# State-space branch ahead of the attention branches, a slot table for the weights, and two modulation vectors in one tile

## The reference, cut to what matters

```python
def trunk_layer(x, mod, lp, li, ctx):
    shift1, scale1, gate1, shift2, scale2, gate2 = [mod[:, i, None, :] for i in range(6)]
    h = rmsnorm(x, lp['g_norm1']) * (1 + scale1) + shift1
    mix, new_ctx = token_mixers(h, lp, li, ctx)
    x = x + gate1 * mix
    h2 = rmsnorm(x, lp['g_norm2']) * (1 + scale2) + shift2
    x = x + gate2 * expert_choice_ffn(h2, ...)

def token_mixers(h, lp, li, ctx):
    proj = jnp.einsum('bsd,dn->bsn', h, lp['w_in'])
    # A: dense attention, B: window attention with a sink, C: state space (SSD), D: differential attention
    branches = jnp.stack([ya, yb, yc, yd], axis=2)
    up = jnp.einsum('bsnw,nwd->bsnd', branches, lp['w_br'])
    g = jax.nn.sigmoid(gate.reshape(Bz, S, N_BRANCH, D_MODEL))
    out = jnp.einsum('bsd,de->bse', jnp.sum(g * up, axis=2), lp['w_out'])
```

## Time and profile before

| what | us |
|---|---|
| median of three runs | 2039.87 (2039.13 to 2042.09) |
| the profiled execution, its own time | 2045.24 |
| its span | 2043.5 |
| PE busy | 1894.9 (93% of the span) |
| DVE, ACT busy | 482.6, 351.9 |
| mean granted TensorE clock | 0.97 |

### The profile page before, as it was taken

One profiled execution on the slowest core, in us unless ns is written; L12 is line 12 of the kernel. 1 busy time (PEld: TensorE's weight loads), 2 busy tenths in 40 slices (PEclk: granted clock), 3 DMA queues, 4 the chain that ended last, 5 costly groups with the idle time before them and its releaser, 6 DMA issues.

```text
span 2043.5 us, 19689 instructions
## 1 busy us (share of the span) xinstructions
PE 1894.9 (93%) x7750; PEld 866.6 (42%) x7750; DVE 482.6 (24%) x1249; ACT 351.9 (17%) x916; POOL 50.1 (2%) x91
## 2 busy tenths in 40 slices
PE   6999999999799999898879999999897999999988
PEld 2464444455333433333345644444554334334322
DVE  1033224453411111101020522243524001111101
ACT  2123222421210100100021232223213001001000
POOL 2100000000300000000000000000000000000000
PEclk8999999988899999999989999999888999999999
DMA  9142113245589999999951411133436899999997
GB/s 379 62 158 79 49 55 124 73 179 204 224 339 418 420 428 429 428 428 428 423 231 62 175 62 62 42 124 135 178 143 247 346 426 424 428 428 428 427 429 308
DMA packets 65476, 532.98 MB, mean 261 GB/s; under 512 B 6688, under 2 KB 6816, under 8 KB 41344
## 3 DMA queue, kind: packets, MB, share of 16 engines
q1 hardware_dynamic: 62256, 527.59, 63.1%
q0 software_dynamic: 3152, 4.47, 0.7%
HBM read 529.16 MB, written 2.88 MB: 260 GB/s over the span
## 4 chain that ended last, share of the span: by engine, by line
PE 77%; DMA 15%; DVE 4%; ACT 2%; issue 1%; SPq 0%; ACTq 0%; DVEq 0%
PE bank L588 73%; DMA ring<-in_w_e 14%; PE bank L597 4%; DMA ring<-in_w_ada 1%; ACT scr L1413 1%; DVE x L1919 0%; DVE scr L1624 0%; DVE hT L1487 0%; DVE scr L1856 0%; DVE scr L1853 0%; DVE hT L1485 0%; DVE scr L1794 0%; ACT scr L1400 0%; ACT scr L1402 0%; DVE scr L1788 0%
## 5 line engine op out<-in xcount | busy, mean ns | idle before, releaser
L588 PE MATMUL bank<-ring,hT 128*128 128x512 f32 (+2 forms) x1440 | 597.2, 568 | 2.6 <-DVE hT L1487 2.6
L588 PE MATMUL bank<-ring,scr 128*64 128x512 f32 (+1 forms) x2176 | 529.2, 598 | 44.6 <-DMA ring<-in_w_e 26.3
L588 PE MATMUL bank<-scr 128*64 128x512 f32 (+6 forms) x2048 | 437.2, 520 | 8.1 <-DVE dsm L1763 4.7
L588 PEld LDWEIGHTS bank<-ring,hT 128*128 128x128 f32 x1440 | 268.0, 191 | 270.6 <-issue 264.4
L588 PEld LDWEIGHTS bank<-ring,scr 128*64 128x64 f32 (+1 forms) x2176 | 176.0, 142 | 368.7 <-issue 310.3
L588 PEld LDWEIGHTS bank<-scr 128*64 128x64 f32 (+3 forms) x2048 | 183.0, 164 | 260.6 <-issue 252.2
L597 PE MATMUL bank<-cst,scr 128*128 128x128 f32 (+1 forms) x530 | 94.7, 294 | 47.8 <-ACT scr L1413 24.9
L1411 ACT ACTIVATE scr<-bank 128x512 f32<-128x512 f32 x32 | 19.1, 597 | 674.6 <-PE bank L588 674.6
L1904 DVE TENSOR_TENSOR scr<-scr,bank 128x512 f32<-128x512 f32 x32 | 22.0, 687 | 470.0 <-ACT scr L1411 470.0
L597 PEld LDWEIGHTS bank<-cst,scr 128*128 128x128 f32 (+1 forms) x530 | 63.2, 159 | 111.6 <-issue 76.1
L588 PE MATMUL bank<-ring,csw 128*32 128x512 f32 x384 | 61.1, 782 | 28.4 <-DMA ring<-in_w_ada 17.7
(11 more groups left out here) (217 smaller groups left out, 1037.8 us busy)
## 6 DMA issues: line engine op xcount, KB each, us to landing
ring<-in_w_e SPq DMA_DIRECT2D x124, 2048.0 KB, 18.8
scr<-in_w_e SPq DMA_DIRECT2D x64, 2048.0 KB, 17.6
ring<-in_w_ada SPq DMA_DIRECT2D x24, 2048.0 KB, 9.7
ring<-in_w_in SPq DMA_DIRECT2D x20, 2048.0 KB, 7.8
ring<-in_w_br SPq DMA_DIRECT2D x8, 1024.0 KB, 7.1
ring<-in_w_out SPq DMA_DIRECT2D x4, 2048.0 KB, 8.6
ring<-in_w_in SPq DMA_DIRECT2D x4, 1552.0 KB, 15.9
ring<-in_w_in SPq DMA_DIRECT2D x4, 1536.0 KB, 6.7
```

Source lines behind the costliest of these rows:

```text
L588: ins = pe.matmul(out, lhsT, rhs, start=start, stop=stop, **kw)
```

## The change

The state-space work goes between the projections and the attention, mixed with projection tiles of A and B. The modulation rows 2 to 5 stand there too. Rows 0 and 1 are accumulated into one tile (the conditioning vectors are in columns 0 and 1 of the 32 for one and 2 and 3 for the other), with one `columns(0)` for both; rows 3 and 4 have a tile each, which DVE adds, with one `columns(3)`. Slots come from a table; the order of branches is C, A, B, D, each lift one pass later than its attention, the last two back to back. The norm of D's output stands inside `lift(2)` on DVE, between the copies of `boT` and the six `up` tiles.

```diff
+ORDER = (("ada", 0), ("ada", 1), ("C", 0), ("D", 0), ("ada", 3), ("AB", 0), ("ada", 4), ("ada", 5), ("gate", 0), ("ada", 2),
+         ("gate", 1), ("lift", 0), ("lift", 1), ("gate", 2), ("lift", 2), ("gate", 3), ("lift", 3), ("out", 0))
+HOME = {("ada", 0): 0, ("ada", 1): 2, ("C", 0): 0, ("D", 0): 2, ("ada", 3): 0, ("AB", 0): 0, ("ada", 4): 2, ("ada", 5): 2,
+        ("gate", 0): 2, ("ada", 2): 0, ("gate", 1): 0, ("lift", 0): 2, ("lift", 1): 3, ("gate", 2): 0, ("lift", 2): 2,
+        ("gate", 3): 0, ("lift", 3): 3, ("out", 0): 0}
-BRANCH = (0, 1, 3, 2)
+BRANCH = (2, 0, 1, 3)
...
                 sp.wait_ge(ssm_out, (li + 1) * 64)
                 sp.sem_inc(dummy_sp, 1)
+                for s in (2, 3):
+                    half(s, 0)
+                sp.wait_ge(kv_out, (li + 1) * 64)
+                sp.sem_inc(dummy_sp, 1)
                 sp.wait_ge(big, BIG_AT[("up", 3, NT - 1, 1)] + 1)
-                for s in (4, 5, 0, 1, 2, 3):
+                for s in (4, 5, 0, 1):
                     half(s, 0)
...
+                def condition(k, second):
+
+                    return csw[:, k, 0:32] if second else csw[:, k, 2:34]
...
                 def columns(v):
-                    taken(("row", v, 1))
+                    taken(("row", 4 if v else 0, 1))
                     b = bank(("col", v))
                     for k in range(KD):
-                        mm(b[:, 2 * k:2 * k + 2], quads(rsb[:, v % 2, :], k) if v > 2 else rsb[:, v % 2, k * P:(k + 1) * P], c_("sel"),
+                        mm(b[:, 4 * k:4 * k + 4], quads(rsb[v], k) if v else rsb[v][:, k * P:(k + 1) * P], sel16[:, 0:4],
                            signal=big if k == KD - 1 else None)
...
+                ab_unit(0)
+                decays(0)
+                ab_unit(1)
+                state_scores(0)
+                decays(1)
+                for h in range(2):
+                    rows(4, h)
+                ab_unit(2)
+                state_products(0)
+                state_scores(1)
+                decays(2)
                 columns(3)
+                ab_unit(3)
+                state_products(1)
+                state_scores(2)
+                for h in range(2):
+                    rows(5, h)
+                ab_unit(4)
+                state_products(2)
+                ab_unit(5)
+                pe.wait_ge(h_in, 1)
+                carried(1)
+                carried(2)
...
+                gate0(0)
+                gate0(1)
+                for h in range(2):
+                    rows(2, h)
+                pe.wait_ge(d_ready, 1)
+                for t in range(NT):
+                    b = bank(("dT", t))
...
+                b = bank(("cdT",))
...
+                b = bank(("ckT",))
...
+                for s in range(2, 5):
+                    gate0(s)
+                pe.wait_ge(ab_ready, 1)
...
+                gate0(5)
...
                         if 1 <= n <= NIT:
                             gate(i + 1, (n - 1) // 2, (n - 1) % 2)
-                        if i == 2 and n >= NIT:
-                            rows(2, n - NIT)
                     if i < 2:
                         scores(i + 1, 0)
                         lift(i)
+                lift(2)
                 lift(3)
-                columns(4)
...
-                for h in range(2):
-                    rows(5, h)
                 widths("h2T")
```

On ACT, ahead of the attention:

```diff
+                gate(0, 0)
+                for t in range(NT):
+                    act.wait_ge(u_ready, t + 1)
+                    A(Mt.rearrange("p j l -> p (j l)")[:, 256 * t:256 * (t + 1)], sz[:, t, :], ACT.Square,
+                      accum_out=st[:, 5, t:t + 1]).then_inc(act_sq, 1)
+                root(NT)
+                gate(0, 1)
+                for h in range(2):
+                    rows(2, h)
+                act.wait_ge(d_ready, 1)
+                act.wait_ge(big_act, taken_by(("ab", NT - 1, 1))[1])
+                for t in range(NT):
+                    if t >= 2:
+                        act.wait_ge(sq_free, NT + t - 1)
+                    A(tmp[:, t % 2, :], AB[:, t, :, :].rearrange("p b n -> p (b n)"), ACT.Square).then_inc(act_sq, 1)
...
```

On DVE, the norm of D's output:

```diff
+                def d_out_norm():
+
+                    dve.wait_ge(o_ready, 3 * NIT)
+                    sqs[0] += NIT
+                    dve.wait_ge(act_sq, sqs[0])
+                    y = rsqrt(st[:, 5, 0:12], 12, HD)
+                    link(V.tensor_scalar(y, y, r_("onemlam"), None, ALU.mult))
+                    b4 = bo[:, :, :].rearrange("p t (h n) -> p (t h) n", n=HD)
+                    link(V.tensor_tensor(b4, b4, rep(y, 2, HD), ALU.mult))
+                    V.tensor_tensor(b4, b4, rep(r_("gdout"), 1, 12), ALU.mult).then_inc(bo_ready, 1)
+
+                lift(2, d_out_norm)
                 lift(3)
-                columns(4)
```

More of the change, by code:

```diff
@@ new lines, in _ @@
+                for t in range(NT):
+                    tokens(bank(("dv", t))[:, 0:ND_ - 512], t, AT_D, slice(512, ND_), signal=big, free=t == NT - 1)
+                pe.wait_ge(dt_done, 1)
+                b = bank(("cum",))
+                for t in range(NT):
+                    o = t * 16
+                    mm(b[:, o:o + 4], c_("upto"), la[:, t, 0:4])
+                    mm(b[:, o + 4:o + 8], c_("from"), la[:, t, 4:8])
+                    mm(b[:, o + 8:o + 16], c_("ones"), la[:, t, :], signal=big if t == NT - 1 else None)
@@ new lines, in _, with ab_unit @@
+                b = bank(("h0T",))
+                for d in range(2):
+                    turn(b[:, d * P:(d + 1) * P], ch("ssm")[:, d * P:(d + 1) * P], signal=big if d else None)
+                def ab_unit(n):
+                    t, br = AB_UNITS[n]
+                    if n == 0:
+                        need(AT_AB)
+                        need(AT_AB + 1)
+                    tokens(bank(("ab", t, br))[:, :], t, AT_AB, slice(br * 512, br * 512 + 512), signal=big,
+                           free=n == len(AB_UNITS) - 1)
@@ new lines, in decay @@
+                def decay(t):
+                    if t == 2:
+                        act.wait_ge(mt_ready, 1)
+                    for d in range(2):
+                        b = grab(("dec", t, d))
+                        for h in range(4):
+                            ins = A(E[t % 2][:, 4 * d + h, :], b[:, h * P:(h + 1) * P], ACT.Exp,
+                                    bias=nacs[:, t, 4 * d + h:4 * d + h + 1])
+                        gave(("dec", t, d), ins)
+                root(48)
+                ab_unit(0)
@@ L1244, in gate @@
+                decay(0)
+                ab_unit(1)
+                decay(1)
+                ab_unit(2)
+                act.wait_ge(sty_ready, 1)
+                A(sst[:, :, :], banks[4][:, 0:256].rearrange("p (i n) -> p i n", i=4), ACT.Copy).then_inc(st0_taken, 1)
+                decay(2)
+                ab_unit(3)
+                for h in range(2):
+                    rows(5, h)
+                ab_unit(4)
+                ab_unit(5)
                 def gate(i, s):
                     t, h = s // 2, s % 2
-                    if s == 0 and i == 2:
+                    if s == 0 and i == 1:
+                        act.wait_ge(ssm_out, (li + 1) * 64)
+                    elif s == 0 and i == 2:
```

774 lines of the change are left out of this document (369 added, 405 removed).

## The result

The changed kernel takes 2020.35 us (2020.02 to 2021.71, 4 runs) against 2039.96 for the kernel before (2039.13 to 2042.09, 4 runs): a ratio of 0.9904, 95% interval 0.9886 to 0.9921. It is 19.6 us faster. Run again later as a control beside other kernels it gave 0.9915 (0.9897 to 0.9933). A few executions of variants ran far longer than the rest (one that was profiled at a mean granted clock of 0.74), and no time here is taken from them.

A forecast was written before the change was run, and what follows sets the result against it. PE was taken as busy nearly all the time except in the state-space stage (76.8 us, 6.9 idle, clock 0.86). Second layer -1.6, first 0, on the median 2039.87: 2038 us, range 2025 to 2052.

The forecast's parts named there:

- The two last lifts: `lift(2)` and `lift(3)` behind the attention: 32.5 us in all, with a 4.5 wait and `lift(3)` at 13.2.
- The start: Start of a layer: one `columns` call less, 2.3, but a 1.2 wait for ACT's copy, so -1.1 us.
- The `columns` call that leaves, and the clock behind it: End of the old state-space stage: the call priced at 2.3 us, the slow clock behind it at 0.7.
- Front: Projections, state space and rows, second layer: 192.6 work, 3.4 waits, 3.2 for two clock falls; 199.2 us, before 149.8.
- The wait at `ckT`: In the front: PE waits 2.4 us for ACT's copy of `dT`, with one clock fall of 1.6 assumed.
- Attention: Three attention passes, second layer: 216.7 less `rows(2)` 4.1, slow entry 1.6 and two short waits 0.5, so 210.5 us.
- `mT` and gate rows: Behind the last lift: these ran slow behind `columns(4)`, and with a wait there instead gain 0.7 us.
- Router: Behind the output projection: with `rows(5)` gone PE waits nearly 6 us and the transposes run slow, +1.3.
- Experts and queues: Expert stage and DMA loads: moved loads change nothing, 0; expert stage 457 to 460 us, no DMA-ended wait in the front.
- the clock holds: Rival, chance 0.28: no slow stretch in the front or `lift(3)`, 6.5 us per layer gained, 2025.
- The clock falls at every light stretch: Rival, chance 0.26: five falls in the front instead of two, each 1.6 us, +4.8 per layer, 2048.
- The rule that was weighed: Array clock: slow by default and after idle, released by activity; by it the front falls only at `ckT`, 2028.

The follow-up runs named there:

- experiment 2: The changed kernel, unchanged, measured again as a control with a second trace: 2023.05 us, ratio 0.9915 against the kernel before.
- Experiment 7: The changed kernel with the matmuls of `columns(0)` at a layer's start issued twice: 2030.18 us, ratio 0.9947 against the kernel before.
- Experiment 10: The changed kernel with four copies added on ACT ahead of the square root of D's norm: 2027.55 us, ratio 0.9938 against the kernel before.
- experiment 5: The kernel before with row vectors of `columns(3)` and `columns(4)` written so weight loads read neighbouring elements: 2033.47 us, ratio 0.9964 against the kernel before.
- experiment 8: The changed kernel with `rows(5)` back behind the output projection, its weights, bias row and first expert's loads in old order: 2012.05 us, ratio 0.9862.

## Why the prediction was wrong

**The step that failed** is the pricing of what stands around the slow stretches: three terms of the sum were taken from rows of before without the wait, the slow clock or the way of reading that was in them. By the table above the forecast had 0.8 per layer and the traces show some 11.

1. *The two last lifts*, 32.5 forecast and 27.3 measured in the second layer, the largest miss. The wait ahead of `lift(3)` was put at 4.5 with D's norm at 5.9, and 2.42 of those were DVE's wait for a root of ACT that the change moves. It measured 2.17. And `lift(3)` was priced slow, 13.2; it measured 10.57 at 16 of 22 places.
2. *The start*, 1.1 forecast, 3.7 and 2.5 measured in the two layers. The slow clock behind two calls was put at nothing.
3. *The `columns` call that leaves, and the clock behind it*, 0.7 forecast from `mT` on, 2.8 measured. "Two `columns` took 4.52, so one is 2.3" was read from `columns(0)` and `columns(1)`, which read neighbouring elements. The call that leaves is `columns(4)`, which reads every fourth: 3.67, and that at full clock too, for in the control of experiment 2 the tile right behind such a call of 3.67 took 7.11. The earlier trace rows had that number. I had passed it over as an effect of the slow clock, though the window that I quoted, 1498 to 1500 in the earlier trace rows, lies behind the call and not in it. The call also slowed `mT` and the gate rows, 2.5 and 0.3. So `columns(4)` held 3.67 + 2.5 + 0.3, less the 1.5 of DVE's last merge that it covered: 5.0 per layer. The forecast had 2.3 and 0.7 for it, less 1.6 for the merge: 1.4.

The remaining 1.8 per layer is the expert stage, which no run ties to the change.

**Point by point.**

- *Start.* One call less and the wait of 0.82 for ACT's copy (forecast 1.2) are as said. What was missed is the clock: in the kernel before it fell during the second call (4.5 for what takes 3.8 at the rate of the changed kernel's) and the transposes behind ran at 5.3, where the profile after has 3.2 and most traces of changed kernels 4.3 to 5.4. Experiment 7 puts some 2 per layer of clock back.
- *Front.* 199.2 forecast, 199.1 to 199.4 in three of the four places and 196.2 in the fourth. It came out right as a sum, but not in its parts: in the second layer of the profile after 2.25 of waits instead of 3.4, and 2.8 + 1.7 = 4.5 of slow clock instead of 3.2. As the call that left was priced 1.4 too low, the work in the front was put 1.4 too high. D's norm was read as 14 us from 1159.0 to 1171.9, which is 12.9; it stayed covered, so nothing hung on it. The wait at `ckT` was forecast at 2.4 and is there; a fall behind it was assumed and is there. The other fall was given to "one of the others"; it was `columns(3)`.
- *Attention.* 210.5 forecast, 210.7 measured in the profile after.
- *Two last lifts.* 32.5 forecast, 27.3 measured. Half of the miss is the wait ahead of `lift(3)`. ACT's square root stood behind the two copies of `rows(2)`, and `rows(2)` is one of the steps that the change moves away. In the profile after DVE waits 0.28 and the norm takes 3.8 instead of 5.9. Experiment 10 shows the two waits tied one for one. The other half is `lift(3)` itself. The one of before stood behind a wait, slow rows and a strided call; the new one stands behind `lift(2)` and a wait. Which of these made the difference wasn't separated.
- *`mT` and gate rows.* -0.7 forecast, -2.8 measured, by experiment 5 the work of `columns(4)`.
- *Router.* A wait of nearly 6 and +1.3 forecast, 5.3 and 1.2 to 1.5 measured. `rows(5)` was forecast as a loss in full, and experiment 8 gives it: some 5 us per layer.
- *Experts and queues.* 457 to 460 in the second layer forecast, 457.5 and 459.3 measured. No DMA ends a PE wait in the front. Both held.
- *Rivals.* The measured time is nearest to "the clock holds" (0.28, 2025), and for part of its reason: it held in `lift(3)` at most places and at `mT`, at the start at 7 of 22 places, and not in the front. The forecast assumed two falls of 1.6 in the front without naming the second; the profile after has two, of 2.8 and 1.7, and the second layer of the other trace has one. That the front came out at 199.2 to the tenth is luck. "The clock falls at every light stretch" is refuted: `decays`, `rows` and `GT` products, 1.0 to 3.6 us each, ran at full rate in the front of the profile after. In the changed kernels the front's slow records stood behind two things: the strided call (12 of 18 places) and the wait of 2.25 at `ckT`, which follows rows and transposes (16 of 20).
- *The rule that was weighed.* The Trainium skill, TensorE: Matmul & The Clock Gate, Part 1, says that activity releases the array's clock. The forecast set the clock of 0.50 with PE 2.00 of 2.00 us busy against it. That window lies right behind 3.67 us of weight loads with 2 columns of output each, during which PE's record is busy throughout. With that call at 1.84 the clock read 1.00 over the same transposes (experiment 5). So the window is no evidence against the rule, and no run here shows what counts as activity.

**What is not settled.** The spans of the two pairs of traces differ by 22.7 on the mean, the medians by 17 to 20. The expert stage's 1.8 per layer, which moves by 3 between executions, could hold the difference, and so could the start. Why `lift(3)` is slow at all six places in kernels of the kind before and at 6 of 22 in the changed ones wasn't separated. Why the tile behind a strided call is slow at 12 of 18 places and not at all of them, and why the wait at `ckT` brought nothing when it went, wasn't tried further.

## What to carry to other kernels

A duration belongs to an operand layout and not only to a shape: where two groups of the same name and shape differ by a factor of two, look at how their operands are read before putting it down to the clock. A stretch on an engine that is carried over as a price must be stripped of its waits first, and of those above all that end on a step which the change itself moves. Fill under a wait is free and the same work in a full stretch is not, so a row that is moved "early" costs its whole length.

## What was not expected of the hardware

- Fifteen fp32 weight loads of 128 x 128 take 1.75 us when each reads 128 neighbouring elements per partition, 3.58 when it reads every fourth.
- Moving that stride to the side that writes, in steps of 128 elements, costs ACT 1.1 instead of 0.60 us per copy of 128 x 512 and DVE 1.09 instead of 0.69 per sum.
- PE's record can be busy for 2.00 of 2.00 us and the granted clock fall all the same: behind a call of 3.67 us that is weight loads with 4 columns each it read 0.50, and the full tile behind took 8.5 to 10.2 us instead of 7.1 at 12 of 18 places. Behind the same call at 1.84 us it did so at 0 of 6.
- What a wait of 2.2 us does depends on what stands ahead of it. Behind the full matmuls of `lift(2)` slow records followed at 6 of 22 places; behind rows and transposes, at `ckT`, at 16 of 20. A wait of 3.6 behind full matmuls was followed by them at both places.
